# Four gated-linear-attention heads: outputs by token, small matmuls padded to 128 rows, squares on four column groups

## The reference

```python
def odd_layer(h, s0, has_meta, pre_g, post_g, w_in, wa2, ba, norm_g, w_out):
    z = rms_norm(h, pre_g) @ w_in                     # boundary: squares, rstd
    q, k, v, gate, lr = jnp.split(z, ODD_SPLITS, axis=-1)
    g = jax.nn.log_sigmoid((lr @ wa2 + ba)) / GLA_TAU # lr has 16 columns
    ...
    o = rms_norm(o, norm_g).reshape(B, T, GLA_VW) * jax.nn.silu(gate)
    h = h + rms_norm(o @ w_out, post_g)

def step(state, xs):                                  # gla_scan, per chunk
    qc, kc, vc, gc = xs
    b = jnp.cumsum(gc, axis=2)
    o_inter = jnp.einsum('bhtd,bhde->bhte', qc * jnp.exp(b), state)
    ...
    o = o_inter + jnp.einsum('bhts,bhse->bhte', scores, vc)
    state = (jnp.exp(b_last)[..., None] * state
             + jnp.einsum('bhsd,bhse->bhde', kc * jnp.exp(b_last - b), vc))
```

## Time and profile before

| | us |
|---|---|
| median of 3 runs | 2025.7 (2025.2 to 2025.81) |
| the profiled execution | 2029.64 |
| its span (first to last instruction) | 2027.7 |
| PE busy, and its share | 1961.5, 97% |
| DVE, POOL, ACT busy | 835.6, 689.0, 641.9 |

### The profile page before, as it was taken

One profiled execution on the slowest core, in us unless ns is written; L12 is line 12 of the kernel. 1 busy time (PEld: TensorE's weight loads), 2 busy tenths in 40 slices (PEclk: granted clock), 3 DMA queues, 4 the chain that ended last, 5 costly groups with the idle time before them and its releaser, 6 DMA issues.

```text
span 2027.7 us, 38550 instructions
## 1 busy us (share of the span) xinstructions
PE 1961.5 (97%) x15065; PEld 1845.0 (91%) x15065; DVE 835.6 (41%) x1469; ACT 641.9 (32%) x1156; POOL 689.0 (34%) x304
## 2 busy tenths in 40 slices
PE   6999999999999999999899999999999999989999
PEld 6998998899889988999779989988998899879999
DVE  5366338534852676000351365054406532650003
ACT  5132223222321324222242343233324422442213
POOL 2333233233323322545314224323342333224551
PEclk8999999999999999999899999998999899979999
DMA  6554345434533453532234453434344424544232
GB/s 203 164 163 129 103 116 158 124 91 126 168 106 97 134 152 117 157 88 84 82 103 116 125 159 92 126 120 162 84 126 146 138 82 120 177 137 133 84 93 96
DMA packets 357436, 252.55 MB, mean 125 GB/s; under 512 B 15135, under 2 KB 324784, under 8 KB 356720
## 3 DMA queue, kind: packets, MB, share of 16 engines
q1 hardware_dynamic: 316194, 186.70, 32.1%
q10 hardware_dynamic: 41070, 63.46, 9.3%
HBM read 213.62 MB, written 36.96 MB: 124 GB/s over the span
## 4 chain that ended last, share of the span: by engine, by line
PE 85%; DVE 8%; issue 4%; ACT 2%; DMA 1%; POOL 0%; ACTq 0%; DVEq 0%; SPq 0%; POOLq 0%
PE proj L1003 70%; PE scratch L1003 9%; PE score L1003 3%; PE scratch L1006 2%; DVE kv L1551 1%; PE proj L1006 1%; DVE xlo L1425 1%; DVE xlo L1423 1%; DVE ek L1822 1%; DVE probw L1579 1%; DVE el L1818 0%; DVE tz L1412 0%; DVE sall L1554 0%; DMA xin<-in_x_prompt 0%; ACT ek L862 0%
## 5 line engine op out<-in xcount | busy, mean ns | idle before, releaser
L1003 PE MATMUL proj<-xhi,wlo 128*128 128x268 f32 x4096 | 1198.3, 293 | 17.2 <-DVE xlo L1425 7.5
L1003 PE MATMUL proj<-xlo,whi 128*128 128x268 f32 x4096 | 1187.1, 290 | 0.0
L1003 PE MATMUL proj<-xhi,whi 128*128 128x268 f32 x4096 | 1186.9, 290 | 0.0
L547 POOL TENSOR_TENSOR wlo<-wraw,whi 128x1024 fp32r<-128x1024 f32 x258 | 635.5, 2473 | 1101.3 <-ACT whi L613 1101.3
L1003 PEld LDWEIGHTS proj<-xhi,wlo 128*128 128x128 f32 x4096 | 787.2, 192 | 38.8 <-issue 23.1
L1003 PEld LDWEIGHTS proj<-xlo,whi 128*128 128x128 f32 x4096 | 786.5, 192 | 0.7
L1003 PEld LDWEIGHTS proj<-xhi,whi 128*128 128x128 f32 x4096 | 783.4, 191 | 0.0
L613 ACT ACTIVATE whi<-wraw 128x1024 fp32r<-128x1024 f32 x258 | 265.0, 1046 | 381.1 <-PE proj L1003 275.6
L1730 DVE TENSOR_SCALAR mix<-proj,cols 128x536 f32 x32 | 24.8, 775 | 341.2 <-ACT te L619 177.8
L1412 DVE TENSOR_TENSOR tz<-proj,rstd 128x536 f32<-128x536 f32 x72 | 51.3, 713 | 236.4 <-PE proj L1003 235.4
L728 ACT ACTIVATE probw<-score,small 128x128 f32<-128x128 f32 (+3 forms) x64 | 33.2, 523 | 173.7 <-DVE small L1502 173.7
(11 more groups left out here) (286 smaller groups left out, 1756.5 us busy)
## 6 DMA issues: line engine op xcount, KB each, us to landing
wraw<-in_w_in SPq DMA_DIRECT2D x192, 512.0 KB, 4.1
wraw<-in_w_out SPq DMA_DIRECT2D x64, 512.0 KB, 4.1
kv<-in_cache_k SPq DMA_DIRECT2D x128, 128.0 KB, 2.3
kv<-in_cache_v SPq DMA_DIRECT2D x128, 128.0 KB, 2.3
sst<-in_state_gla ACTq DMA_DIRECT2D x32, 512.0 KB, 4.9
out<-sst ACTq DMA_DIRECT2D x32, 512.0 KB, 3.5
hbuf<-h_residual ACTq DMA_DIRECT2D x2, 4288.0 KB, 14.8
vb<-v_sample_rows ACTq DMA_DIRECT2D x32, 256.0 KB, 5.5
```

The costliest lines, as they stand in the source:

```text
L547: pool.tensor_tensor(wlo[:, slot, :, 0:width], wraw[:, kc, :, 0:width], whi[:, slot, :, 0:width].bitcast(F32), ALU.subtract).then_inc(s_lo, 1)
L1003: return pe.matmul(out, lhsT, rhs, start=start, stop=stop, skip_group_check=True)
```

## The change

Three edits, all around the GLA heads.

1. *Token-major outputs.* OC takes `ed` and `st` as weights and moves the state and gv, 512 columns wide, so a piece's output has tokens on the partitions; it lies in `score`, the half that B doesn't use, in three matmuls instead of twelve. ACT (`token_rows`) then squares it with a running sum, takes Ln and Exp for 1/rms per token, and copies it scaled into `orow`. One chunk later PE transposes orow (TR0 to TR4), and `o_rows` copies that into og. The sample rows do the same (`sample_outputs` in the middle of chunk 23, TR5). SO, SS0 to SS2, the squares over features, POOL's and DVE's adds and the multiplication by r go away, and DVE's last step is one operation per v.
2. *128 rows.* The last piece's keys go to `kdt`, 128 rows of which 112 are zero, and SU4 uses all rows of it and of gv; `lrT` and `wa2` have 128 rows with zeros below the 16.
3. *Squares on four column groups.* At the boundary the squares of two k are summed together, after the projections of the odd one, by four matmuls of 32 columns of ones (two k times two halves), each in its own column group of `score`. At the end ACT copies the sum (`gsum`) and PE spreads it by two matmuls with a constant (`spread`) before `finish_rms(2)`. `square` comes one k later in ACT's code.

```diff
@@ HEAD_PLAN
-    16: "SK0 B0", 17: "OC0 SU00 SU01 SK1", 18: "OC1 SU10 SU11 B2 SK2",
-    19: "OC2 SU20 SU21 SK3", 20: "OC3 SU30 SU31 B4 SK4", 21: "OC4 SU40 SU41",
-    22: "B6", 23: "SO SS0 SS1 SS2",
+    16: "SK0 B0", 17: "OC0 SU00 SU01 SK1", 18: "TR0 OC1 SU10 SU11 B2 SK2",
+    19: "TR1 OC2 SU20 SU21 SK3", 20: "TR2 OC3 SU30 SU31 B4 SK4", 21: "TR3 OC4 SU40 SU41",
+    22: "TR4 B6", 23: "TR5",
...
+HEAD_JOBS = [x for x in HEAD_OPS if x[0] != "B" and x[:2] != "OC"]
@@ ACT, boundary
-                square(2, k % 2, k, mix[:, k, :])
+                if k:
+                    square(2, (k - 1) % 2, k - 1, mix[:, k - 1, :])
+            square(2, 1, KT - 1, mix[:, KT - 1, :])
+            act.wait_ge(s_acc, 2 * KT)
+            act.copy(gsum, score[:, 0:TH]).then_inc(s_gsum, 1)
@@ ACT, head
+                def token_rows(c):
+                    w = P if c < TT else (TAIL if c == TT else NB)
+                    o, total, root = score[0:w, GV:2 * GV], stat[0:w, 16 + c:17 + c], stat[0:w, 24 + c:25 + c]
+                    act.wait_ge(s_otok, 6 * s + c + 1)
+                    chain.link(act.activation(orow[0:w], o, ACT.Square, accum_out=total))
+                    chain.link(act.activation(root, total, ACT.Ln, scale=1.0 / GV, bias=eps[0:w]))
+                    chain.link(act.activation(root, root, ACT.Exp, scale=-0.5))
+                    act.activation(orow[0:w], o, ACT.Copy, scale=root).then_inc(s_orow, 1)
@@ ACT, per chunk
-                        o_rows(c - 17)
+                        if c > 17:
+                            o_rows(c - 18)
                         if c < 21:
+                            act.wait_ge(s_otok, 6 * s + c - 16)
                             decay_start(c - 16)
+                        token_rows(c - 17)
@@ PE, boundary
-                pe.wait_ge(s_sq, KT + k + 1)
-                for a in range(2):
-                    last = matmul(score2[:, a, 0:TH], ones, (tz, te)[k % 2][:, a, :], start=k == 0, stop=k == KT - 1)
...
+                if k % 2:
+                    pe.wait_ge(s_sq, KT + k + 1)
+                    for a in range(2):
+                        for j in range(2):
+                            r = 32 * (2 * j + a)
+                            last = matmul(score[r:r + 32, 0:TH], ones[:, 0:32], (tz, te)[j][:, a, :], start=k == 1, stop=k == KT - 1)
+                    last.then_inc(s_acc, 2)
+            pe.wait_ge(s_gsum, 1)
+            for a in range(2):
+                last = matmul(score2[:, a, 0:TH], spread[:, a, :], gsum)
+            last.then_inc(s_ss, 1)
@@ PE, head
+                def token_outputs(c):
+                    w = P if c < TT else TAIL
...
+                    if 6 * s + c:
+                        pe.wait_ge(s_orow, 6 * s + c)
+                    o = score[0:w, GV:2 * GV]
+                    if c:
...
+                        for j in range(2):
+                            matmul(o, ed[:, j, 0:w], state[:, j, :], start=j == 0, stop=False)
+                    matmul(o, st[0:w, 0:w], gv[0:w, c, :], start=c == 0, stop=True).then_inc(s_otok, 1)
+                def sample_outputs():
+                    pe.wait_ge(s_srow, s + 1)
+                    pe.wait_ge(s_orow, 6 * s + TT + 1)
+                    matmul(score[0:NB, GV:2 * GV], fold, srow).then_inc(s_otok, 1)
...
-                            last = matmul(o, gv[0:w, c, vc], st[0:w, 0:w], start=c == 0, stop=True)
+                        pe.wait_ge(s_orow, 6 * s + c + 1)
                         for v in range(4):
+                            last = transpose(out[:, v * w:(v + 1) * w], orow[0:w, v * P:(v + 1) * P])
...
-                        done(matmul(out[:, 0:GV], kd[0:w, j * P:(j + 1) * P], gv[0:w, c, :]))
+                        done(matmul(out[:, 0:GV], (kd if c < TT else kdt)[:, j * P:(j + 1) * P], gv[:, c, :]))
@@ DVE, end of a head
-                dve.wait_ge(*ro_ready.at("head", "o", s))
-                r = ek[:].rearrange("p j t -> p (j t)")[:, 0:T]
+                dve.wait_ge(*free_a.at("head", f"TR{TT + 1}", s))
                 for v in range(4):
-                    link(dve.scalar_tensor_tensor(out=og[:, v, :], in0=og[:, v, :], scalar=cols[:, GN + v:GN + v + 1], in1=r, op0=ALU.mult, op1=ALU.mult))
                     m = tile_at(mix, 4 * s + v)
-                    last = dve.tensor_tensor(m, m, og[:, v, :], ALU.mult)
+                    last = dve.scalar_tensor_tensor(out=m, in0=og[:, v, :], scalar=cols[:, GN + v:GN + v + 1], in1=m, op0=ALU.mult, op1=ALU.mult)
```

More of the change, by code:

```diff
@@ L352, in build @@
         ybuf = sb1("ybuf", [P, 11, 4, P])
+        spread, gsum = ybuf[:, 0, 0:2, :], acc[:, 0:TH]
         stage.close()
@@ L358, in build @@
         srow = tef[:, 0:GV]
[L359 to L360 removed]
+        lrT = sb1("lrT", [P, T])
+        wa2 = sb1("wa2", [P, GK])
         gq = sb1("gq", [P, 2, T])
@@ L372, in build @@
         og = sb1("og", [P, 4, T])
+        orow = sb1("orow", [P, GV])
         refs = sb1("refs", [P, 2, 17])
@@ L941, in head @@
                     if c == 22:
+                        o_rows(TT)
                         act.wait_ge(*free_d.at("head", "SU41", s))
                         act.dma_start(gla_prompt[0, bass.ds(s, 1)].rearrange("o (j p) v -> p (o j) v", p=P), state[:]).then_inc(s_gout, 16)
-                        act.wait_ge(s_so, 8 * s + 8)
-                        for v in range(4):
-                            last = act.activation((gq, gk)[v // 2][:, v % 2, 0:TP], og[:, v, 0:TP], ACT.Square)
-                        last.then_inc(s_gsq, 1)
+                token_rows(TT + 1)
                 if last_head:
                     x_hi("out1", 0, 2)
-                act.wait_ge(*free_d.at("head", "SO", s))
-                for v in range(4):
-                    last = act.activation((gq, gk)[v // 2][:, v % 2, TP:T], og[:, v, TP:T], ACT.Square)
-                last.then_inc(s_gsq, 1)
-                r = ek[:].rearrange("p j t -> p (j t)")[:, 0:T]
-                def norm_log(a):
-                    lo_t, hi_t = SS_COLS[a]
-                    act.wait_ge(*full.at("head", f"SS{a}", s))
-                    act.activation(r[:, lo_t:hi_t], bank_of("head", f"SS{a}")[:, 0:hi_t - lo_t], ACT.Ln, scale=1.0 / GV, bias=eps).then_inc(s_fa, 1)
-                norm_log(0)
-                norm_log(1)
+                o_rows(TT + 1)
                 if last_head:
@@ L967, in head @@
                     x_hi("out1", 5, 7)
-                norm_log(2)
-                act.wait_ge(*free_a.at("head", "SS2", s))
-                act.activation(r, r, ACT.Exp, scale=-0.5).then_inc(ro_ready.sem, 1)
             with act.Fori(0, GH - 1) as s:
@@ L1006, in transpose, with chunk @@
                 return pe.transpose(out, x, ident[0:x.shape[0], 0:x.shape[0]])
-            def chunk(n, par, kc):
+            def chunk(n, par, kc, between=None):
                 if kc == 0:
@@ L1021, in chunk @@
                         last = matmul(out, whi[:, slot, k, :], xhi[:, kt, x], start=False, stop=kt == KT - 1)
+                    if a == 0 and between:
+                        between()
                 if kc == 1:
@@ L1292, in run @@
                         last.then_inc(s_so, 2)
+                        return
+                    if kind == "OC":
+                        token_outputs(int(op[2]))
                         return
@@ L1320, in run @@
                         done(last)
-                    elif kind == "OC":
+                    elif kind == "TR":
                         c = int(op[2])
-                        w = P if c < TT else TAIL
-                        pe.wait_ge(*free_d.at("head", f"SK{c}", s))
-                        pe.wait_ge(*free_a.at("head", "VT13", s))
-                        if c:
-                            pe.wait_ge(*ed_ready.at("head", str(c), s))
-                            pe.wait_ge(*free_d.at("head", f"SU{c - 1}1", s))
-                        for v in range(4):
-                            o, vc = out[:, v * w:(v + 1) * w], slice(v * P, (v + 1) * P)
-                            if c:
-                                for j in range(2):
-                                    matmul(o, state[:, j, vc], ed[:, j, 0:w], start=j == 0, stop=False)
-                            last = matmul(o, gv[0:w, c, vc], st[0:w, 0:w], start=c == 0, stop=True)
+                        w = P if c < TT else (TAIL if c == TT else NB)
+                        pe.wait_ge(s_orow, 6 * s + c + 1)
+                        for v in range(4):
+                            last = transpose(out[:, v * w:(v + 1) * w], orow[0:w, v * P:(v + 1) * P])
                         done(last)
@@ L1337, in run @@
                         c, j = int(op[2]), int(op[3])
-                        w = P if c < TT else TAIL
-                        done(matmul(out[:, 0:GV], kd[0:w, j * P:(j + 1) * P], gv[0:w, c, :]))
-                    elif op == "SO":
-                        pe.wait_ge(s_srow, s + 1)
-                        for v in range(4):
```

(14 more changed lines are left out.)

65 lines of the change are left out of this document (26 added, 39 removed).

## The result

The changed kernel takes 1991.69 us in the median (1990.17 to 1995.85) beside 2025.45 of the kernel before; the ratio is 0.9837 (95% interval 0.982 to 0.9854). That is 33.8 us less, where 27.3 were forecast; the time lies in the range given. In two later comparisons the unaltered changed kernel gave 0.9815 (0.9783 to 0.9847) and 0.9833 (0.982 to 0.9847).

A forecast was written before the change was run, and what follows sets the result against it. PE, busy 97% of the span, was taken to bound the kernel; -14.8 - 4.5 + 1.3 - 6.1 - 3.2 = -27.3 us took the median from 2025.7 to 1998, range 1987 to 2013.

The forecast's parts named there:

- A: Heads, behind the 16-token chunk (OC4, SU4): four low-clock stretches, 33.6 us at .44 per us, go; -14.8 us.
- B: Start of heads 0 to 2, behind G: three low-clock stretches of 3.40 us go; -4.5 us (0 to -5.1).
- C: PE's instructions in the heads at full clock, work removed against work added: +1.3 us in all (-1 to +4).
- ACT's cover: Heads: ACT's new 2.1 us of work per chunk has 8 us before the transposes need it, so PE does not wait.
- D: Boundary: column groups let DVE's 1.95 us per x_lo set the pace, with a 3.9 us tail; -6.1 us.
- E: Start of out1: DVE's og·r and mix become one operation, .80 less for each of four; -3.2 us.
- 2: Heads, 16-token chunk: thin work and transposes lower the clock again, losing 7.4 or 14.8; 2005 to 2013 us, chance .18.
- 3: Boundary gives nothing: column groups run one after another or the tail exceeds the gain; 2004 to 2008 us, chance .08.
- 4: Heads, steps 18 to 23: ACT's rows chain is late and PE waits at the transposes; slower, 2036 us, chance .05.
- 5: Whole kernel: nets to nothing, low clock stays and the boundary loses; 2025 us, chance .03.
- the loss of 1.6: G in the heads: if 16 rows take as long as 128, padding saves no instruction time; 1.6 us worse.

The follow-up runs named there:

- su4_16_rows: Changed kernel with SU4 back on 16 rows of kd and gv, all else as changed; ratio 0.9864 to the kernel before.
- boundary_alone: Kernel before with only the boundary edit (squares on four column groups, copy, spread); ratio 0.9963 to the kernel before.
- padding_alone: Kernel before with only the 128-row padding of SU4 and G, OC4 still twelve 16-column matmuls; ratio 0.9940 to the kernel before.
- rows_plus_4: Changed kernel with four more Squares in each token_rows chain on ACT; ratio 0.9945 to the kernel before.
- changed_again: Changed kernel unaltered, timed and profiled a second time; ratio 0.9815 to the kernel before.
- token_major_alone: Kernel before with only the token-major outputs, no padding and the boundary as before; ratio 0.9898 to the kernel before.
- tr_twice: Changed kernel with the four transposes of every TR job issued twice; ratio 0.9873 to the kernel before.
- ones_wide_pairs: Changed kernel with the boundary's sums on 128 columns of ones, without column groups, copy and spread; ratio 0.9884 to the kernel before.
- g_16_rows: Changed kernel with G back on 16 rows of wa2 and lrT, all else as changed; ratio 0.9834 to the kernel before.

## Why the prediction came out right, and where its sum was off

- **A, the clock behind chunk 4, -14.8:** right in mechanism. The low stretches are gone in every profile of the changed kernel, and those of A and B together, 43.8 us at the measured .44 to .47, are worth 19 to 21 beside the 19.3 forecast. The step that named the cause was too simple: the prediction gave OC4's columns and SU4's rows together and could not tell them apart; the runs show that each of them suffices to let the clock fall in some heads. Its price of .44 compared SU4 at the low clock with SU1, another job. SU4 with 16 rows at full clock takes 1.91 (su4_16_rows), which makes .48 of SU4's 3.69; over whole heads .44 to .47 was measured, so the number held.
- **B, the clock behind G, -4.5:** the amount came out, but two thirds of it by luck. The prediction put all three short stretches of the earlier trace rows behind G, at the start of heads 0 to 2. Only that of head 0 is there. The other two stand at the start of heads 2 and 3, directly behind SO and SS and more than 10 us ahead of G. Head 2 begins at 1420.75, and these are the two stretches and PE's rows around the first:

```profile
1420.40:1423.80 3.40, 3.40 (x16) 3.40 (x17) 1.66 (x3) 2.20 (x4) 0.00 (x0) 0.50 0.57 156
1611.60:1615.00 3.40, 3.40 (x17) 3.40 (x17) 2.19 (x3) 2.84 (x6) 0.63 (x1) 0.51 0.59 154
...
1417.25 0.95 PE L1003 MATMUL scratch<-lower,te 128*128 128x8 f32 x8
...
1420.36 0.54 PE L1003 MATMUL scratch<-gq,both 128*128 128x8 f32 x2 [1.03 <-DVE gq L1918]
...
1434.17 1.17 PE L1003 MATMUL scratch<-lrT,wa 16*128 16x268 f32 x4
```

  What runs ahead of them are the 8-column matmuls of SO and SS2 and a wait of 1.03, which edit 1 takes away; the padding of G ends one stretch of the three. Whether edit 1 is what ended the two was not tested: they come behind two of the first three heads before, behind one in boundary_alone, and behind none in padding_alone, which keeps SO and SS.
- **C, PE's work, +1.3:** this is the term that was mis-sized. The heads gained 24.3, so without the clock some 3 to 5 us less rather than 1.3 more. OC1 to OC3 cost 2.58 each where 2.85 was taken (a matmul of 512 columns is .86 in a row of three, not .95), OC4 2.78 where 3.15 was; G saves .5 instead of .4 per head; against it SU11's wait only halved. Added up over the timeline this is -1.3 per head in heads 0 to 2 and +1.6 in head 3, -2.3; some 2 us of the heads' gain are not split further.
- **ACT's cover:** right for the changed kernel. The 8 us hold for TR0 to TR4; TR5, which the prediction counted among the same places, has only half a chunk, and rows_plus_4 shows that the cover breaks first there and at B6.
- **D, the boundary, -6.1:** -7.1 measured, of which .3 is an earlier first x_lo, so the stage itself gave 6.8; and the steps held: x_lo every 1.95, a group of four .59 to the next start (.66 taken), from the last group's start to the split 3.66 (3.9 taken, from the end of the projections), then 3.61 (3.6). The last two blocks came faster, 1.3 each, as DVE has no more sums to make for them. Part of the 6.8 is chance: in the profiled execution of before the granted clock stayed at 0.50 for 6.7 us from the first x_lo on, in that of the changed kernel for 3.7. Where it did so for alike times the difference is smaller: 45.4 before against 39.3 in changed_again (6.7 and 6.6) is 6.1, and 44.1 in padding_alone and token_major_alone, whose boundary is that of before, against 38.6 (3.9 and 3.7) is 5.5.
- **E, out1, -3.2:** -4.1. The one operation per v gave 3.0, as forecast (from the first of these operations to the x_lo behind the last, 8.6 before and 5.6 after). The other 1.1 lies ahead of it. What was not seen: POOL's adds held up its wlo, which then ran beside DVE's first x_lo. The rows of before, POOL and DVE, and one of after:

```profile
1798.11 1.32 POOL L595 TENSOR_TENSOR gq<-gq,gk 128x528 f32<-128x528 f32 x1
1799.39 2.36 POOL L547 TENSOR_TENSOR wlo<-wraw,whi 128x1024 fp32r<-128x1024 f32 x1
...
1800.15 2.16 DVE L1423 TENSOR_TENSOR xlo<-mix,xhi 128x536 fp32r<-128x536 f32 x1
...
1782.13 2.89 DVE L1432 TENSOR_TENSOR xlo<-mix,xhi 128x536 fp32r<-128x536 f32 x1
```

  This x_lo took 2.16 where each of the five takes .65 after the change, and it ended .56 after POOL's wlo. The last row shows that the same is still to be had: of the last six x_lo, which PE waits for, two take 2.89 and 2.87 in both kernels, each beside one of two wlo, and end .6 after it.
- **The rivals:** 2 did not come, and tr_twice speaks against its mechanism. 3 did not come; ones_wide_pairs is what it would have looked like, 9.7 us worse. 4 and 5 did not come. The padded G did save PE's time, .6 us per head, so the loss of 1.6 that the prediction set beside C did not come either.

## What to carry to other kernels

A stretch of low clock while the engine is fully busy was here a sign of thin work just ahead of it, and thin was few rows or few columns; look, stretch by stretch, at what ran just before and at both of its operands, and expect that mending one side only makes the fall rarer. Where sums are made in 32 columns, column groups free PE only down to the pace of the next engine (here DVE's 1.95 us instead of PE's 2.38), and what was overlapped before (here the rms step) lands on the path: move what does not need its result ahead of it. Cover for added work is counted at each reader, and the last, shortest one breaks first.

## What was not expected of the hardware

- A 16-row matmul of 268 columns took longer than a 128-row one: in g_16_rows the two pairs of G made a head .6 us longer, and the record of a pair is 1.17 before where the ones-matmul of the same columns is 1.07. SU4 with 16 rows takes 1.91 to the next chunk's start, 1.42 with 128, but most of that comes back in the chunk behind it (6.11 and 6.44). Whether the rows themselves or the change to them and back costs the time is open.
- The length of the low stretches differs from execution to execution of the same code (34 and 43.8 us in heads that are alike), and with it the time: the kernel before spread from 2013.8 to 2030.9 in one comparison of 14 executions, where the prediction took .6 us from three; the changed kernel spread over 9 us at most, in four or five. That the clock is the whole of that spread was not shown; layer 0 varies too.
- VectorE's x_lo took .65 us by itself and 2.2 to 2.9 when POOL subtracted beside it; each of the five in the two kernels ended some .6 us after a subtraction of POOL. No run varied this by itself.
